# The scaled diagonals of a gather-and-sum kernel: from one ScalarE copy per slot to one VectorE operation per slot

## The reference, cut to what matters

```python
idx = jnp.take_along_axis(cand_i, best_pos, axis=-1)
gate = jax.nn.softmax(best_s, axis=-1)
u = expert_u[idx]
act = jax.nn.gelu(jnp.einsum('nhkd,nd->nhk', u, xb, preferred_element_type=jnp.float32), approximate=False)
coef = (gate * act).astype(xb.dtype)
return jnp.einsum('nhk,nhkd->nd', coef, expert_v[idx])
```

## Time and profile before

| | us |
|---|---|
| median of 3 runs | 1772.76 |
| lowest, highest | 1769.74, 1774.85 |
| the profiled execution, its time | 1769.74 |
| its span, first to last instruction | 1767.9 |
| outside the span | 1.8 |

### The profile page before, as it was taken

How to read it: one execution, slowest core, us unless ns; L and a number is a source line. 1 busy time by engine, 2 the same in 40 slices (tenths; PEclk the granted TensorE clock), 3 DMA queues, 4 the chain that set the end, 5 groups by cost and what they waited for, 6 DMA issues and landing times.

```text
span 1767.9 us, 22280 instructions
## 1 busy us (share of the span) xinstructions
PE 1232.3 (70%) x7384; PEld 597.0 (34%) x7384; DVE 1193.6 (68%) x3381; ACT 495.8 (28%) x1139; POOL 606.5 (34%) x588
## 2 busy tenths in 40 slices
PE   6846687675766788696866559869885766655654
PEld 3533222222333466343233327634431333211111
DVE  2379856655889766767368987667854879945554
ACT  1123212411223344362112334334511213311111
POOL 1032253452422333333333223224333334355442
PEclk9978798897888899797988779979988869778776
DMA  8489799999989899898999679999989979999996
GB/s 339 155 355 361 300 414 421 422 424 417 415 346 364 325 412 424 353 418 353 423 406 387 271 298 401 424 399 374 421 370 422 418 313 398 409 403 422 421 421 270
DMA packets 84069, 666.97 MB, mean 377 GB/s; under 512 B 9376, under 2 KB 9520, under 8 KB 10880
## 3 DMA queue, kind: packets, MB, share of 16 engines
q0 software_dynamic: 74464, 540.13, 75.3%
q1 hardware_dynamic: 9216, 124.50, 17.0%
q10 hardware_dynamic: 288, 1.05, 0.1%
HBM read 664.59 MB, written 1.05 MB: 377 GB/s over the span
## 4 chain that ended last, share of the span: by engine, by line
PE 28%; DMA 28%; DVE 27%; issue 10%; ACT 5%; POOL 1%; POOLq 0%; ACTq 0%; DVEq 0%; SPq 0%; PEldq 0%
DMA ring<-in_experts,idx_now 27%; PE acc L743 14%; DVE ring L1271 9%; PE act_bank L490 4%; PE dve_bank L476 3%; DVE scratch L938 2%; PE act_bank L676 2%; ACT diag L907 2%; DVE scratch L1181 1%; DVE scratch L1182 1%; DVE scratch L1184 1%; DVE scratch L1180 1%; DVE h L1298 1%; ACT scratch L778 1%; DVE scratch L1183 1%
## 5 line engine op out<-in xcount | busy, mean ns | idle before, releaser
L1271 DVE CUSTOM_DVE_ANT_0 ring<-ring,hn 128x1024 f32<-128x1024 f32 x512 | 624.6, 1224 | 356.7 <-DMA ring<-in_experts,idx_now 338.9
L743 PE MATMUL acc<-ring,diag 64*64 64x512 f32 x4096 | 635.7, 748 | 318.9 <-ACT diag L907 309.5
L418 POOL DMA_INDIRECT ring<-in_experts,idx_now x512 | 579.2, 1131 | 787.0 <-PE acc L743 636.5
L743 PEld LDWEIGHTS acc<-ring,diag 64*64 64x64 f32 x4096 | 157.7, 158 | 670.5 <-ACT diag L907 430.1
L900 ACT ACTIVATE acts<-dots 128x2 f32<-128x2 f32 x256 | 52.0, 203 | 887.2 <-DVE dots L1271 877.9
L490 PEld LDWEIGHTS act_bank<-hnT,wbuf 128*128 128x128 f32 x1920 | 235.6, 203 | 80.3 <-issue 63.5
L490 PE MATMUL act_bank<-hnT,wbuf 128*128 128x128 f32 x1920 | 248.7, 290 | 18.9 <-DVEq L295 13.4
L907 ACT ACTIVATE diag<-cst,coefs 128x64 f32<-128x64 f32 x512 | 150.3, 340 | 226.7 <-DVE coefs L1279 174.6
L413 POOL COPY idx_now<-idx 128x8 uint32 x64 | 21.8, 341 | 324.7 <-PE acc L743 258.0
L778 ACT ACT_TABLE_LOAD x82 | 105.2, 1283 | 12.6 <-DMA rowc<-in_rows 8.0
L476 PE MATMUL dve_bank<-wbuf,scratch 128*128 128x512 f32 x192 | 93.2, 621 | 4.0 <-DMA wbuf<-in_weights 2.4
(11 more groups left out here) (112 smaller groups left out, 847.0 us busy)
## 6 DMA issues: line engine op xcount, KB each, us to landing
wbuf<-in_weights SPq DMA_DIRECT2D x56, 2048.0 KB
ring<-in_experts,idx_now POOLq DMA_INDIRECT x512
kept<-in_weights SPq DMA_DIRECT2D x2, 2048.0 KB, 15.0
gains<-in_gains SPq DMA_DIRECT2D x2, 512.0 KB, 12.5
scratch<-in_bias POOLq DMA_DIRECT2D x1, 1024.0 KB, 7.4
gains<-in_gains ACTq DMA_DIRECT2D x2, 512.0 KB, 10.7
out<-h SPq DMA_DIRECT2D x2, 512.0 KB, 8.1
scratch<-in_bands POOLq DMA_DIRECT2D x1, 768.0 KB, 5.1
```

Source lines behind the costliest of these rows:

```text
L418: pool.indirect_dma_start(ring[:, s], None, io[f"experts{layer}"], bass.IndirectOffsetOnAxis(idx_now[:, j * RING + s:j * RING + s + 1], 0) ...
L743: last[rows] = pe.matmul(acc[rows][half][home:home + HALF_P], diag[part, n % DIAGS], ring[part, n % RING, D + half * CW:D + (half + 1) * C ...
L1271: dve.tensor_tensor_reduce(out=ring[:, slot, 0:D], in0=ring[:, slot, 0:D], in1=hn[:, phase % NBLK], scale=1.0, scalar=0.0, op0=ALU.mult, o ...
```

## The change

ScalarE's `make_diagonals` and the tile `coefs` go. VectorE gets a `make_diagonals` in the place of `coefficients`: for each slot of the pair one SCALAR_TENSOR_TENSOR, (`folded` times the slot's `acts` column) times the slot's `gate` column, the latter broadcast over the 64 elements. The wait for the Gelu stays on VectorE, and the two waits for `pairs_summed` move there from ScalarE. TensorE still waits for `diag_ready`.

```diff
-        coefs = sb("coefs", BODY)
...
-            def make_diagonals(g, q):
-                act.wait_ge(sem("coef_done"), g * GROUPS + (q + 1))
-                for rows in range(2):
-                    act.wait_ge(sem(f"pairs_summed{rows}"), g * GROUPS + (q + 1 + AHEAD - DIAGS // GROUP))
-                for s in range(GROUP):
-                    ins = act.activation(diag[:, (q * GROUP + s) % DIAGS], folded, ACT.Copy,
-                                         scale=coefs[:, q * GROUP + s:q * GROUP + s + 1])
-                ins.then_inc(sem("diag_ready"), 1)
...
-                    if n % GROUP == GROUP - 1:
-                        make_diagonals(g, q)
...
-            def coefficients(phase, g, q):
+            def make_diagonals(phase, g, q):
                 dve.wait_ge(sem("gelu_done"), g * GROUPS + (q + 1))
-                cols = slice(q * GROUP, (q + 1) * GROUP)
+                for rows in range(2):
+                    dve.wait_ge(sem(f"pairs_summed{rows}"), g * GROUPS + (q + 1 + AHEAD - DIAGS // GROUP))
                 at = g * BODY + (q * GROUP - phase // NBLK * NBLK * SLOTS)
-                dve.tensor_tensor(coefs[:, cols], acts[:, cols], gate[:, bass.ds(at, GROUP)],
-                                  ALU.mult).then_inc(sem("coef_done"), 1)
+                for s in range(GROUP):
+                    n = q * GROUP + s
+                    ins = dve.scalar_tensor_tensor(diag[:, n % DIAGS], folded, acts[:, n:n + 1],
+                                                   gate[:, bass.ds(at + s, 1)].to_broadcast([P, HALF_P]),
+                                                   ALU.mult, ALU.mult)
+                ins.then_inc(sem("diag_ready"), 1)
```

More of the change, by code:

```diff
@@ L1288, in experts @@
                     if n % GROUP == GROUP - 1:
-                        coefficients(phase, g, n % BODY // GROUP)
+                        make_diagonals(phase, g, n % BODY // GROUP)
                 b = phase % NBLK
```

## The result

The changed kernel takes 1778.05 us in the median (1773.95 to 1783.22, 13 runs), the kernel before 1767.46 us (1762.12 to 1774.85, 13 runs). The ratio is 1.0059, with a 95% interval of 1.0043 to 1.0074: slower by 10.4 us (7.6 to 13.1). The forecast was +7.2. The median of before lies under the 1772.76 of the first three runs, so the forecast's 1780.0 is nearer to the measured time than its difference is. Its 95% interval is 2 to 5 us to either side, and that of a difference between two changed kernels, each timed beside the kernel before, is 3 to 5 us. One execution of the kernel before and one of eight_waits_kept took 1797 us at a granted TensorE clock of 0.75, against 0.84 to 0.86 in all the others, and both are left out of the differences.

A forecast was written before the change was run, and what follows sets the result against it. VectorE bounds the routing stretches, DMA most others. Routing +9.3, dense mixer passages +2, one before 973 us +0.5, ScalarE -4.2, end -0.35 give +7.2: median 1772.76 to 1780.0, range 1766 to 1793.

The forecast's parts named there:

- VectorE as the bound beside the routings: In four stretches where routing runs beside the slots, VectorE, about 90% busy, sets the pace; lost time isn't won back.
- The price of the operation: Each new 128x64 operation on VectorE takes 278 ns; a pair costs +0.31 us, between +0.20 and +0.40.
- The four stretches: Routing stretches at 103, 509, 973 and 1426 us grow by 2.8, 1.9, 2.1 and 2.5 us, together +9.3.
- the cover: In the routing stretches, VectorE's existing waits hide new work: -1.2, -0.9, -0.9, -0.9, and in the last 3.4 us more.
- What moves to VectorE's queue: The waits for `pairs_summed` move to VectorE; counted 0 because TensorE is busy there, up to 7.7 us in the range.
- the third rival: VectorE held by TensorE: the moved wait stops dots too, 7.7 us on top of the sum, 1787.7; chance 0.07.
- What goes from ScalarE: ScalarE's two copies and an engine crossing go; ending late diagonals at four places gives -4.2 us, the path's end -0.35.
- the 1.6 us at 591 us: TensorE idles 1.59 us while ScalarE makes late diagonals; with VectorE writing them this idle time goes, -1.6.
- the second rival: Faster: ScalarE, no longer waiting behind VectorE's ticks, empties TensorE's banks earlier; needs more than 12.5 us, 1760 at 20; chance 0.18.
- signs of being wrong: Wrong if routing stretches don't grow, the operation costs over 0.3 us start to start, or stretches with TensorE busy get shorter.
- The sum: Over the whole kernel, 9.3 + 2 + 0.5 - 4.2 - 0.35 = +7.2 us.
- the shorter path: A diagonal is ready some 0.35 us earlier, counted at holes in the DMA in the routing stretches and once at the end.

The follow-up runs named there:

- eight_waits_kept: Changed kernel with eight diagonals instead of four, VectorE still executing both waits, on the pair four before: ratio 1.0044, or 1.0027 without the 1797 us execution.
- price_alone: Kernel before, with two more 128x64 operations on VectorE behind each product, written to an unread tile; ScalarE still makes the diagonals: ratio 1.0115, +20.3 us.
- price_twice: Changed kernel with two more 128x64 operations a pair on VectorE, written to an unread tile: ratio 1.0156, +27.6 us against the kernel before.
- wait_alone: Kernel before, with VectorE also waiting for both sums of the pair two before ahead of its product: ratio 1.0037, +6.5 us.
- eight_diagonals: Changed kernel with eight diagonals instead of four and VectorE's waits for the sums of pairs removed: ratio 1.0012, +2.1 us against the kernel before.
- copies_beside: Changed kernel with ScalarE still making two 128x64 Copies a pair into an unread tile, without waiting for VectorE: ratio 1.0042, +7.4 us against the kernel before.
- scalar_held: Changed kernel with ScalarE still waiting for the pair's diagonals at the old place but making nothing: ratio 1.0091, +16.1 us against the kernel before.
- price_gone: Changed kernel with one 128x2 product a pair instead of the two 128x64 operations, only each diagonal's first column written: ratio 0.9927, -12.9 us against the kernel before.

## Why the prediction was right, and where it was not

**VectorE as the bound beside the routings: right.** 71 of the 256 pairs carry the loss (+12.6), the others a gain (-5.7), and price_alone and price_twice give nearly the same slope, +20.3 and +17 for 0.39 us a pair. Scaled to the 0.32 of the change that is some 14 to 17 us.

**The price of the operation: right**, 0.32 against 0.31 us a pair, 282 against 278 ns.

**The four stretches: the term was too small**, +9.3 forecast and +15.8 in the trace. Part of that is the moved wait, 1.2 + 1.1 + 1.6 + 0.3 = 4.2 us in wait_alone's trace, though eight_diagonals, without it, is only 2.3 us shorter there. The rest, 11.6, compares with 57 x 0.31 = 17.7 before the cover. The last stretch gave +5.5 instead of +2.5: I had let VectorE's 3.4 us of waiting for rows hide as much again.

**"What moves to VectorE's queue": wrong.** The step counted 0, because TensorE's sum rarely comes last, and where it does TensorE is busy, so that a later dot costs nothing. It came last 4 times, 4.5 us, near the 6 times of the earlier trace rows. But the wait cost 6.5 us alone, and 8.3 us in the changed kernel. By eight_waits_kept the larger part, some 5.6 us, is of the kind that the step put at nothing, VectorE held by TensorE; all 4 times lie away from the routings, 4.3 of the 4.5 us in the rows of the scan. The step left out a second part, that waits are work of VectorE's sequencer: 26 gaps of about 0.24 us instead of 0.15 behind the operation of line 930 alone, and with the like gaps behind others some 2.7 us beside the routings. This is the mechanism of the third rival at about its price (7.7 us), though not where the rival looked for it. The waits of the changed kernel:

```profile
DVE diag L1270 <- ACT acts L899: 40.9, 134, 1.3
...
DVE diag L1270 <- DVE scratch L930: 6.3, 26, 0.3
...
DVE diag L1270 <- PE acc L742: 4.5, 4, 2.1
```

**"What goes from ScalarE": the right sign, the wrong place.** Of the 1.6 us at 591 us nearly nothing came. The same place in the changed kernel:

```profile
600.88 1.97 PE L497 MATMUL act_bank<-cst,hn 128*128 128x128 f32 x8
...
602.03 0.60 ACT L777 ACTIVATE hnT<-act_bank 128x512 f32<-128x512 f32 x1 [2.30 <-PE act_bank L497]
...
602.95 0.60 ACT L777 ACTIVATE hnT<-act_bank 128x512 f32<-128x512 f32 x1 [0.32 <-PE act_bank L497]
...
603.60 0.21 PEld L742 LDWEIGHTS acc<-ring,diag 64*64 64x64 f32 x8 [1.15 <-ACT hnT L777]
603.60 1.95 PE L742 MATMUL acc<-ring,diag 64*64 64x512 f32 x16 [0.75 <-ACT hnT L777]
```

TensorE idles there 0.75 us (1.59 before) for ScalarE's second copy of the transposes, which its own ticks need, diagonal or not. From the start of the transposes to TensorE's next sum it is 603.60 - 600.88 = 2.72 us, and 594.70 - 591.83 = 2.87 before, so 0.15 us is won. The busy time of ScalarE's copies is worth nothing (copies_beside); what their lateness cost elsewhere no run isolates. What came is the mechanism of the second rival, ScalarE standing behind VectorE's ticks, which I had set to zero in the sum; scalar_held puts it at 5.7 us (1 to 11). It decides nothing by itself, since the rival wanted 12.5. One of the prediction's own signs of being wrong came with it: the stretches with TensorE busy got shorter, by 5.9 and 4.8 us in the mixers of layer 1, of which about half is the change's.

**The sum.** With 14 to 17 for the operations, 6 to 8 for the wait and -6 for ScalarE's queue, 4 to 9 us of gain are left to reach +10.4. Each of these terms is known to a few microseconds, so this remainder is too. It would be the shorter path, for which I had 1.4 and which no run isolates. For it speaks that scalar_held, with ScalarE held and only the path shorter, keeps most of the mixers' -10.7 us in its trace, and that price_gone, with a path shorter still, reaches -12.9 in spite of the wait. So the forecast's +7.2 against +10.4 owes part of its nearness to luck: two steps that were wrong cancelled, a wait taken for nothing and gains taken too small.

## What to carry to other kernels

When work moves to the engine that bounds only some stretches, count the units of work in those stretches and multiply; then try the split, since here the same edit costs 12.6 us in 71 of 256 pairs and gives 5.7 us in the rest. A wait that moves to another engine can cost even when it rarely holds; a buffer deep enough to make it redundant (eight diagonals) took 8.3 of the 10.4 us away. An engine that waits in program order for another's late result holds up everything behind it: look for its long waits in front of an operation on which the fullest engine depends, not at its busy time. And when stretches of two traces are compared, look also at a kernel in which the stretch was left as it was: here it differed by 3 to 7 us from before as well.

## What the runs showed of the hardware that was not expected

- Two more semaphore waits behind an operation that is followed by a wait for itself lengthen the gap to the next operation from 0.15 to about 0.25 us, in the changed kernel and in wait_alone alike, and in eight_waits_kept, where they are always satisfied.
- A per-partition scalar from `acts`, written by ScalarE a moment before, costs no more than one that has long lain there: 282 ns at 64 elements against 345 at 128 fits the 1.05 ns an element of the earlier trace rows.
- ScalarE's two products of 128x1 take 0.62 us, longer than the two diagonals of 128x64 (0.59 us) behind them: in this kernel each product is followed by a wait for itself, and the diagonals are not.
